# Taking 96 unused transposes out of the residual turns of a one-core two-block transformer kernel

## The reference

```python
# first block
u = rms_norm(h, norm_mix_pre);  parts = split(u @ w_in)
y = sigmoid(gate_a) * (nsa(parts) @ w_up_nsa) + sigmoid(gate_b) * (swa(parts) @ w_up_swa)
h = h + rms_norm(y @ w_out, norm_mix_post)                          # update 1
u = rms_norm(h, norm_mlp_pre)
h = h + rms_norm(square(relu(u @ w_mlp_in)) @ w_mlp_out, norm_mlp_post)   # update 2
# second block: mods = silu(c) @ ada_w + ada_b, nine vectors (shift, scale, gate) per layer
x = x + 0.5 * (1 + g) * swiglu(modulate(rms_norm(x)), w_in, w_out)  # layer 0: update 3
x = x + (1 + g) * pool_mixer(modulate(rms_norm(x)))                 # update 4
x = x + 0.5 * (1 + g) * swiglu(...)                                 # update 5
k, v = shared_kv(x)      # modulate(rms_norm(x)) @ w_kv, k normed and rotated
x = x + 0.5 * (1 + g) * swiglu(...)                                 # layer 1: update 6
x = x + (1 + g) * (moba_attention(q, k, v) @ w_o)                   # update 7
x = x + 0.5 * (1 + g) * swiglu(...)                                 # update 8
```

## The kernel before, in words

| place | transposes | stands behind | stands ahead of |
|---|---|---|---|
| turn 2 (line 775) | 18 | the first partition sums | `turn_u` of t = 0 |
| pool (line 1243) | 16 | the last product of ffn0 | the band matmuls |
| turn 4 (line 780) | 8 | the second partition sums | the first product |
| turn 5 (line 782) | 10 | the second partition sums | the first product |
| kv (line 1271) | 12 | the first kv product | `wide8`, which waits for weights |
| turn 6 (line 1291) | 8 | the second partition sums | `turn_u` of t = 1 |
| turn 6 (line 1294) | 10 | `turn_u` of t = 1 | the first product |
| turn 7 (line 782) | 14 | `turn_u` of t = 0 | the first product |

## Time and profile before

### The profile page before, as it was taken

One profiled execution on the slowest core, in us unless ns is written; L12 is line 12 of the kernel. 1 busy time (PEld: TensorE's weight loads), 2 busy tenths in 40 slices (PEclk: granted clock), 3 DMA queues, 4 the chain that ended last, 5 costly groups with the idle time before them and its releaser, 6 DMA issues.

```text
span 1387.4 us, 16653 instructions
## 1 busy us (share of the span) xinstructions
PE 1342.5 (97%) x6785; PEld 1105.5 (80%) x6785; DVE 928.1 (67%) x1012; ACT 656.0 (47%) x849; POOL 24.6 (2%) x49
## 2 busy tenths in 40 slices
PE   8999899999998999998999999999999998999998
PEld 8976577888886888887788888878888886788887
DVE  5467788766668776667776677576666756744454
ACT  5356666545457333445444436453444545644432
POOL 2200000000000000000000000000000000000000
PEclk9999999999999999999999999999999999999999
DMA  9997569677774887773877773667778441455651
GB/s 251 253 330 227 155 239 357 232 275 273 274 270 168 301 288 273 273 242 122 286 272 281 282 273 106 215 224 260 273 276 308 143 133 51 151 194 188 192 184 61
DMA packets 165567, 317.54 MB, mean 229 GB/s; under 512 B 7018, under 2 KB 114852, under 8 KB 156276
## 3 DMA queue, kind: packets, MB, share of 16 engines
q1 hardware_dynamic: 161872, 305.50, 64.7%
q0 software_dynamic: 3440, 10.93, 2.8%
q10 hardware_dynamic: 180, 0.05, 0.0%
HBM read 314.10 MB, written 1.84 MB: 228 GB/s over the span
## 4 chain that ended last, share of the span: by engine, by line
PE 87%; DVE 7%; ACT 3%; issue 2%; DMA 1%; ACTq 0%; SPq 0%; DVEq 0%
PE bank L715 27%; PE bank L717 26%; PE bank L716 26%; PE bank L812 2%; DVE full L1836 2%; PE bank L735 1%; DVE wlo L1769 1%; PE bank L738 1%; DMA raw<-in_w_in 1%; DVE xt L1824 1%; DVE mix L1822 1%; PE bank L762 1%; DMA raw<-in_w_mlp_in 1%; PE bank L1076 1%; ACT whi L1348 1%
## 5 line engine op out<-in xcount | busy, mean ns | idle before, releaser
L1769 DVE TENSOR_TENSOR wlo<-raw,whi 128x2048 fp32r<-128x2048 f32 x205 | 469.2, 2290 | 262.6 <-ACT whi L1348 262.3
L1348 ACT ACTIVATE whi<-raw 128x2048 fp32r<-128x2048 f32 x205 | 392.3, 1914 | 216.3 <-PE bank L717 179.3
L715 PE MATMUL bank<-whi,uhi 128*128 128x512 f32 (+2 forms) x1088 | 429.4, 395 | 12.5 <-DVE ulo L1849 4.6
L717 PE MATMUL bank<-whi,ulo 128*128 128x512 f32 (+2 forms) x1088 | 419.9, 386 | 0.0
L716 PE MATMUL bank<-wlo,uhi 128*128 128x512 f32 (+2 forms) x1088 | 418.8, 385 | 0.0
L715 PEld LDWEIGHTS bank<-whi,uhi 128*128 128x128 f32 x1088 | 206.1, 189 | 60.2 <-issue 17.2
L717 PEld LDWEIGHTS bank<-whi,ulo 128*128 128x128 f32 x1088 | 206.0, 189 | 42.0
L716 PEld LDWEIGHTS bank<-wlo,uhi 128*128 128x128 f32 x1088 | 206.5, 190 | 39.7 <-issue 1.2
L715 PE MATMUL bank<-whi,hsplit 128*128 128x512 f32 (+1 forms) x512 | 200.9, 392 | 1.1 <-DVE wlo L1769 1.1
L717 PE MATMUL bank<-whi,hsplit 128*128 128x512 f32 (+1 forms) x512 | 198.5, 388 | 0.0
L716 PE MATMUL bank<-wlo,hsplit 128*128 128x512 f32 (+1 forms) x512 | 198.3, 387 | 0.0
(11 more groups left out here) (253 smaller groups left out, 1026.0 us busy)
## 6 DMA issues: line engine op xcount, KB each, us to landing
raw<-in_ffn_w_in SPq DMA_DIRECT2D x176, 512.0 KB, 4.8
ada<-in_ada_w SPq DMA_DIRECT2D x72, 1024.0 KB, 7.2
raw<-in_ffn_w_out SPq DMA_DIRECT2D x44, 1024.0 KB, 5.1
raw<-in_w_in SPq DMA_DIRECT2D x16, 1024.0 KB, 10.7
raw<-in_w_mlp_in SPq DMA_DIRECT2D x16, 1024.0 KB, 6.8
raw<-in_w_mlp_out SPq DMA_DIRECT2D x16, 1024.0 KB, 5.0
ada<-in_kv_ada_w SPq DMA_DIRECT2D x8, 1024.0 KB, 7.3
raw<-in_w_kv SPq DMA_DIRECT2D x8, 1024.0 KB, 5.3
```

The lines of the kernel that those rows point to most:

```text
L715: nc.tensor.matmul(o, sh, mh, start=start, stop=False, skip_group_check=skip)
L717: return nc.tensor.matmul(o, sl, mh, start=False, stop=stop, skip_group_check=skip)
L1348: ins = nc.scalar.activation(whi[:, ring(n), :], raw[:, ring(n), :], ACT.Copy)
L1769: ins = nc.vector.tensor_tensor(wlo[:, ring(n), :], raw[:, ring(n), :], whi[:, ring(n), :].bitcast(F32), ALU.subtract)
```

## The change

The eight calls of `keep_busy` in the turns go, 18 + 8 + 10 + 14 + 16 + 12 + 8 + 10 = 96 transposes in all. The 46 at the head stay. No wait, no semaphore and no other instruction of any engine is added, removed or moved; the lines of the changed kernel stand 5 to 9 lower from the first edit on.

```diff
@@ first_chunk(n, e, o)
                 window(e, 0)
-                if e == 2:
-                    keep_busy(18, bank[5])
                 turn_u(e, 0)
                 window(e, 1)
                 if e == 4:
                     pe.wait_ge(x_ready, 16)
-                    keep_busy(8, bank[3])
-                if e in (5, 7):
-                    keep_busy(10 if e == 5 else 14, bank[3 if e == 7 else 6])
                 for t in range(2):
@@ pool
             pe.wait_ge(pool_in, 32)
-            keep_busy(16, bank[7])
             windows(0, 0)
@@ kv
             first_chunk(b, 5, bank[4:6])
-            keep_busy(12, bank[6])
             for q in range(4):
@@ wq
             turn_u(6, 0)
             window(6, 1)
             pe.wait_ge(x_ready, 24)
-            keep_busy(8, bank[3])
             turn_u(6, 1)
             pe.wait_ge(u_lo, 26)
-            keep_busy(10, bank[1])
             for q in range(4):
```

## The result

The changed kernel took 1397.83 us, the median of nine runs (1393.43 to 1401.65). The kernel before, on the same chips, took 1389.17 us (1387.12 to 1392.14). The ratio is 1.0068, 95% interval 1.0055 to 1.0080: 9.4 us slower. I had forecast +4.5 us, 1393.6 us, with a range up to 1397.3. Way and mechanism came as forecast; the size did not.

The account below looks back on a forecast made before the run. TensorE, matmuls busy 97%, was taken to set the time between the turns. Clock losses of 5.26 us less 0.8 us saved gave +4.5 us on 1389.15, so 1393.6 us, range 1390.2 to 1397.3.

Parts of the forecast that it names:

- my 0.8: Total saving from the removal: 0.5 us in turn 5 and 0.3 us in the first group of turn 6.
- My 5.26 us: Total cost of lost clock: turn 2 0.35, turn 4 0.63, turn 5 0.75, kv 1.08, turn 6 1.1, turn 7 1.35 us.
- my 0.44: Turn 2: delay of the chain when the first four transposes run at half pace, before the chance of 0.8.
- my 1.58: Price in us of a 3.4 us low-clock stretch lying wholly over wide work; used for turn 4 with chance 0.4.
- thin stretches: Stretches with no wide work (waits, matmuls of a few columns), taken as what may bring the clock down.
- Between 1.9 (never) and 3.3 us (always) I draw a line: Thin stretches of 1.9 us never lose the clock, of 3.3 us always; chances between are rounded towards the middle.
- the clock stays down: Rival: falls chain, two at each place, giving over 1397 us, up to 1401; chance 0.07.
- The pool stage I had put at 0: Pool stage: a fall ahead of the band matmuls is spent before 638.4; cost 0, at most 1.58 us.
- 0.35 + 0 + 0.63 = 1.0 us: Costs forecast for turn 2 (0.35), the pool stage (0) and turn 4 (0.63).
- turn 6, 0.8: Turn 6: 1.1 us cost from a fall ahead of the q projection, with 0.3 us saved in its first group.
- the waits left do no harm: Rival: few or none of the places lose the clock; 1388.3 to 1391 us; chance 0.18.
- the transposes are on the path: Rival: each place gives back its own transposes' time, 10.6 us at most, 1378.6 us; chance 0.03.

Follow-up runs that it names:

- both profiles of the changed kernel: All 96 transposes gone, profiled in two measurements: first profiled execution 1393.89 us, median 1397.83 us; once more, profiled execution 1396.42 us, median 1398.12 us.
- wide_sums: Kernel before with all transposes, each one-column matmul of the partition sums made 32 columns wide: 1386.42 us, ratio 0.9990.
- no_t7: Kernel before with only the 14 transposes of turn 7 gone: 1390.22 us, ratio 1.0009.
- no_t6: Kernel before with only the 8 and 10 transposes of turn 6 gone: 1390.29 us, ratio 1.0011.
- no_t2_pool_t4: Kernel before with only the 18, 16 and 8 transposes of turn 2, the pool stage and turn 4 gone: 1391.60 us, ratio 1.0020.
- no_t4: Kernel before with only the 8 transposes of turn 4 gone: 1392.42 us, ratio 1.0025.
- no_t5kv: Kernel before with only the 10 transposes of turn 5 and the 12 of the kv stage gone: 1391.85 us, ratio 1.0017.
- narrow: Kernel before with the 96 transposes of the eight places replaced by 48 one-column matmuls (96 instructions): 1398.70 us, ratio 1.0067.
- more_fill: Kernel before with 18 more transposes in turn 1 and 22 more in the pool stage: 1386.46 us, ratio 0.9986.

## Why the prediction was wrong

**Right: the transposes were nearly free.** 78 of them lay in waits that stayed. Turn 7's product starts 4.08 us behind its first transpose with and without them, turn 4's idle time grew from 1.28 to 2.16 us, the kv stage's from 1.56 to 2.85. The other 18 gave back what I had counted. In both profiles of the changed kernel the first product of turn 5 starts 0.5 us sooner behind the turn's first transposes (4.07 and 4.05 us, before 4.53), and the q projection 0.5 us sooner (10.51 and 10.53 us, before 11.00): 0.95 us for my 0.8. What had cost that time was the low clock under them and not the transposes: wide_sums has them all, ran both places at 1.00, and has 4.06 and 10.44 us.

**Right: the loss is in the clock, and about what one us of it costs.** My 5.26 us stood for four new stretches of 3.4 us (the chances 0.8, 0.4, 0.2, 0.8, 0.8 and 1), 13.6 us of low time, at 0.39 us each. Measured were 25 us more low time and 9.4 us, 0.38 each (over all kernels 0.32). The single prices hold where the fall is short: 0.47 us in turn 2 for my 0.44, 1.5 us in turn 4 for my 1.58, 1.6 us in turn 7 in the profile of no_t7.

**Wrong: how much low time there would be.** The step that failed is the one that turned thin stretches into falls: "Between 1.9 (never) and 3.3 us (always) I draw a line", with one stretch of 3.4 us for each fall. It gave four more stretches of 3.4 us; the 25 us that were measured are more than seven. (The first profile has four more than the eight of before, the second seven.) Two things were mis-sized in it.
- Length. Falls of 6.8 us are common and not the exception. Both profiles of the changed kernel have one in turn 7, the first one another in turn 5, no_t6 and no_t2_pool_t4 have them too, and one of 10.2 us stands in the pool stage. In turns 5 and 7 the first half of the fall holds waits and little product (2.04 us busy of 3.30 at 847.4, 1.11 at 1195.5), and the clock is not given back at its end. I had this length as the rival "the clock stays down", gave it 0.07, and held against it that after each fall of before the clock "was back when wide work ran". The trace of before did not bear that out. It has seven falls; the line was drawn from two of them, and one of the others, in turn 1, lasts 6.8 us, its second half over transposes and partition sums of 512 columns:

```profile
232.60:239.40 6.80, 4.49 (x16) 3.36 (x17) 5.55 (x10) 5.46 (x14) 2.09 (x4) 0.50 0.95 367
```

- Places. The pool stage I had put at 0; it loses 1.1 us in the profile of no_t2_pool_t4 and 0.4 in the second one of the changed kernel. The attention behind turn 6, which I did not consider, lost 1.9 us in the first profile of the changed kernel and 0.3 in the second. That the change brings this on is not shown: before falls there too, for 3.4 us, and no_t4, which has all the transposes of turn 6, fell there for 6.8 us and lost 2.0.

By groups: 0.35 + 0 + 0.63 = 1.0 us for turn 2, pool and turn 4 measured 2.8; turn 5 and kv, 1.3 with the saving taken off, measured 2.4; turn 6, 0.8, measured 1.5; turn 7, 1.35, measured 1.3. Turn 7 alone comes out at my figure by its ratio, though its interval reaches 2.8 us. In no_t5kv the loss is larger than 3 us more low time can cost even if all of it lay on products (0.46 us each); that lies within its interval, and falls that move from a wait onto a product would do the same, which no run here tells apart.

**The rivals.** That the waits left do no harm is excluded by the result, and its reason, that idle gaps alone cost the clock, by narrow. That the transposes are on the path is excluded: each part removed alone came out slower or the same, none faster, and the 0.95 us above is all that came back. *The clock stays down* came nearest: the median, 1397.8 us, lies in its "over 1397 us, up to 1401". Its reason was another, that the next wait finds the engine late and falls again; what the traces show is one fall that lasts two stretches.

**Luck.** The nine runs of the changed kernel spread over 8.2 us and the first profile lies at their fast end: +4.7 us in span, close to my 4.5 by chance, since it missed two falls of before that have nothing to do with the change and had none in turns 2 and 4. The time of the one execution that I summed against was a fair base (1389.15 us; the median of 83 later runs is 1388.6), but its falls were one draw of many.

## What to carry to other kernels

Matmuls whose result nobody reads can earn more than they cost: in this kernel 96 transposes, 10.6 us of TensorE of which removing them gave back 1 us, held back 25 us at half clock and 9.4 us of time. Before taking such filler out, or when looking for time in a kernel bound by TensorE, read the granted clock by stretch and look at what runs in the thin places, not at the busy share alone: here it was the same under one-column matmuls and under transposes, and the clock was not. Widening the one-column sums did about as much as 40 more filler transposes and added no instruction, and neither alone was enough in turn 1. Compare such kernels by many runs and by the mean clock of each, since where a fall lands differs from run to run and moves a single profile by several us.

## What the runs showed of the hardware

- One-column matmuls issued back to back, 0.11 us apart, did not hold TensorE's clock although the profile counts them as busy: 96 of them in place of 96 transposes gave 55 us at the low clock against 27. With the partition sums 32 columns wide in place of one the low time was 15 us with the transposes in place and 39 without, against 27 and 52 to 54.
- A fall lasted 3.4, 6.8 or 10.2 us. One whose first 3.4 us ran product matmuls with hardly a wait ended there (turn 4 of the second profile of the changed kernel, turn 7 of no_t7). Most of those that began over a wait of about a us or more lasted 6.8 us (turn 7 of both profiles of the changed kernel), and so did some that began over one-column matmuls or transposes without a wait (turn 1 of more_fill, busy for 6.70 of 6.70 us).
- The clock falls in places that differ between executions of the same kernel. The kernel before ranged from 0.986 to 0.994 in mean clock and from 1386.2 to 1393.4 us.
